# Gate rows of every third quad made one slab earlier, h stores four slabs behind the load, and the input stage's waits and time-step chain moved

## The chip, the cores and the metric

The kernel runs on one core of one Trainium2 chip. The metric is the device time of one execution in microseconds (us). The profile is one execution taken by the hardware profiler. TensorE is called PE, VectorE DVE, ScalarE ACT, GpSimd POOL and SyncE SP; each works through its own list of instructions in order and waits on semaphores.

## The reference, cut to what matters

A block of two layers over 256 tokens of width 2048. Layer 0 mixes with a Mamba-2 (SSD) scan, layer 1 with sliding-window attention; both add attention over a memory of 256 tokens, and both end with a PEER layer that picks 128 of 16384 experts for each token.

```python
for l in range(2):
    if l == 0:
        proj = x @ w_in_a                     # 1536 z | 2560 conv input | 24 time steps | 512 memory queries
        main = mamba2_mixer(...)              # conv, silu; dt = softplus(dt_raw + dt_bias); scan; gate; norm
    else:
        main = sliding_window_attention(...)
    x = layer_norm(ALPHA * x + concat(main, memory_attention(...)) @ w_out[l])
    # PEER
    sc = einsum('bshtd,htkd->bshtk', (x @ peer_wq).reshape(...), subkeys)
    top_s, top_i = top_k(sc, 16)              # twice: for each half, then over the 256 sums
    idx, gate = ...                           # 8 heads x 16 experts for each token
    hid = einsum('td,tkd->tk', x, u[idx])
    act = gelu(hid) * gate
    x = layer_norm(ALPHA * x + einsum('tk,tkd->td', act, v[idx]))
```

## The kernel before, in words

**Slabs and pieces.** All weights come from HBM as slabs of 128 partitions x 2048 f32 (1 MB), each made of two pieces of 1024. Every f32 operand is split into a high and a low part of type fp32r: ACT copies a piece from `raw` into `wh` (`hi`, line 512), DVE subtracts and writes `wl` (`lo`, line 1297), and PE multiplies with both (line 854). `raw` has three slab slots, `wh` and `wl` four piece slots, so `hi(p)` waits until PE has used piece p - 4, `lo(p)` follows `hi(p)`, and PE follows `lo(p)`. SP loads slab n when DVE has split slab n - 3 (line 410). A slab of a "t" stage (`slab_t`) takes 16 pairs of a matmul with `wh` and one with `wl`; in the middle of the next slab PE adds the part that ACT copied into `cross` (`fold`), and only then ACT evacuates the slab from PSUM.

**Stages, in order, with their place in the profile.** Memory keys and values (0 to 105 us, 16 slabs), input projection (117 to 332, 36 slabs), SSD scan and memory attention, output projection, query projection, then the experts of layer 0: 128 U slabs (578 to 1284) and 128 V slabs (1284 to 1868). Layer 1 does the same with its own attention; its U slabs run from 2236 to 2937 and its V slabs to 3523.

**Start of the input stage.** Before it, PE multiplies x with the 24 time-step columns (`dtw_r`) and transposes the memory values (line 1137), ACT copies them out (763, 765), and SP stores them to `kv_scratch` (442, 443), since the output of the input stage (`proj`) takes their place. ACT and DVE wait for that store (`spill_done`) and only then split the first pieces. After 20 of the 36 slabs PE stops to transpose the time steps (line 1144, for which DVE copies PSUM into `dt_c`), and DVE computes the input of softplus (1679 to 1683) and goes on with the convolution (1695, 1698), whose operations alternate with two `lo` each.

**U slabs.** PE computes all 128 hidden values for 192 of the 256 tokens in dense form. The other 64 tokens are done by gathers: POOL gathers rows of u, DVE takes 64 dot products (`dot`, line 1462). The first 64 slabs run beside the top-k search; their outputs (`h_kept`) stay in SBUF. Slabs 64 to 127 form eight trips of eight slabs, the spread stage. Their gelu (line 649) writes `hring`, of which two slots are used here, and SP stores each to `h_scratch` (line 456); gelu of slab k waits for the store of slab k - 2. The dense gates are made there, in 48 quads of four tokens, six quads a trip: DVE builds two one-hot tiles (`hot`, line 1580), ACT multiplies one by the gate (`gate_rows`, four operations, line 663), PE multiplies both (`spread`, when the piece of `Q_PIECE` in the trip has been used), ACT copies the gates out (`gates_out`, line 655), and DVE multiplies the kept hidden values (`gate_kept`, line 1573). `hot` has two slots. In ACT's list for slab s of a trip stand: `cross` of slab s - 1, `hi` of piece 2s + 2, gelu of slab s - 1, `hi` of piece 2s + 3, at most one `gates_out`, at most one `gate_rows`.

```python
Q_PIECE = (2, 4, 7, 10, 12, 15)
GATE_SLAB = tuple((p + 1) // 2 - 1 for p in Q_PIECE)     # 0, 1, 3, 4, 5, 7
STORE_LAG = 5
```

SP issues, for each U slab k, the load of slab k and then the store of slab k - STORE_LAG, which waits for that slab's gelu.

## Time and profile before

| | us |
|---|---|
| device time, median of 3 runs | 3527.97 |
| lowest and highest run | 3519.58, 3531.91 |
| profiled execution, device time | 3539.45 |
| profiled execution, span from first to last instruction | 3537.6 |
| busy in that span: PE, DVE, ACT, POOL | 3378.0, 2786.6, 1914.3, 449.6 |

The mean granted clock of PE in the profiled execution is 0.985 of full speed. The busy time of PE is modelled: its matmuls are pipelined, so the gaps between them are a safer reading than their lengths. In the timeline, a figure in brackets is how long the engine sat idle ahead of a row, and what ended it.

### The profile page before, as it was taken

What the parts mean: (1) busy time and instruction counts of PE and PEld (TensorE: products, weight loads), DVE (VectorE), ACT (ScalarE), POOL (GpSimd) and SP (SyncE); (2) the same over time, 40 slices, a digit from 0 to 9 for tenths busy, and PEclk for the clock granted to TensorE, in tenths of its full rate; (3) what the DMA queues carried; (4) which work ended last, traced back from release to release, by engine and by line L of the source; (5) the groups of instructions that cost most, each with busy time, mean ns of one, the idle gap of its engine ahead of it and who ended that gap; (6) DMA issues with size and microseconds to landing.
All of it is one profiled execution on the core that took longest, in us unless ns stands there. A gap on an engine that the chain in (4) does not pass through costs nothing.

```text
span 3537.6 us, 51772 instructions
## 1 busy us (share of the span) xinstructions
PE 3378.0 (95%) x19476; PEld 3020.1 (85%) x19476; DVE 2786.6 (79%) x3856; ACT 1914.3 (54%) x3350; POOL 449.6 (13%) x264
## 2 busy tenths in 40 slices
PE   9999899999999899999998999999999999999998
PEld 7887678998999888888887777999999998888887
DVE  4455556999898878889886555799988887888997
ACT  4445445554666555555555455555566665555555
POOL 0000000001112112222210000001122121222320
PEclk9999999999999999999999899999999999999999
DMA  6443044678899889999984324568889998999995
GB/s 251 162 169 139 33 169 174 224 275 324 314 348 344 313 299 355 355 361 376 377 333 158 119 81 157 191 220 305 317 327 342 331 337 321 359 351 363 379 382 221
DMA packets 169062, 968.86 MB, mean 274 GB/s; under 512 B 18896, under 2 KB 52688, under 8 KB 55376
## 3 DMA queue, kind: packets, MB, share of 16 engines
q1 hardware_dynamic: 132048, 698.61, 53.2%
q0 software_dynamic: 36864, 268.45, 20.8%
q8 instruction: 70, 1.15, 0.1%
q14 instruction: 80, 0.66, 0.1%
HBM read 951.26 MB, written 15.73 MB: 273 GB/s over the span
## 4 chain that ended last, share of the span: by engine, by line
PE 66%; DVE 20%; DMA 8%; ACT 4%; issue 1%; SPq 0%; DVEq 0%; ACTq 0%
PE ps L854 65%; DVE wl L1297 9%; DMA h_scratch<-hring 7%; DVE arena L1462 3%; ACT wh L512 2%; DMA raw<-in_u 1%; ACT hot L663 0%; DVE arena L1514 0%; DVE arena L1524 0%; DVE arena L1504 0%; DVE arena L1520 0%; DMA arena<-in_v,idx 0%; DVE arena L1499 0%; ACT xx L636 0%; DVE arena L1498 0%
## 5 line engine op out<-in xcount | busy, mean ns | idle before, releaser
L1297 DVE TENSOR_TENSOR wl<-raw,wh 128x1024 fp32r<-128x1024 f32 x1264 | 1525.8, 1220 | 604.4 <-ACT wh L512 601.3
L854 PE MATMUL ps<-xx,wh 128*128 128x384 f32 (+1 forms) x5504 | 1716.6, 373 | 51.8 <-DVE wl L1297 29.2
L512 ACT ACTIVATE wh<-raw 128x1024 fp32r<-128x1024 f32 x1264 | 1333.5, 1057 | 619.8 <-PE ps L854 497.3
L854 PE MATMUL ps<-xx,wl 128*128 128x192 f32 (+1 forms) x5504 | 1424.9, 259 | 0.0
L854 PE MATMUL ps<-wh,act 128*128 128x512 f32 x3584 | 1189.0, 389 | 2.8 <-DVE act L1320 2.8
L854 PEld LDWEIGHTS ps<-xx,wh 128*128 128x128 f32 x5504 | 1038.2, 189 | 122.8 <-DVE wl L1297 36.7
L854 PEld LDWEIGHTS ps<-xx,wl 128*128 128x128 f32 x5504 | 1053.3, 191 | 0.3
L854 PE MATMUL ps<-wl,act 128*128 128x512 f32 x2304 | 897.0, 389 | 0.0
L854 PEld LDWEIGHTS ps<-wh,act 128*128 128x128 f32 x3584 | 673.4, 188 | 143.8 <-DVE wl L1297 3.5
L854 PEld LDWEIGHTS ps<-wl,act 128*128 128x128 f32 x2304 | 432.9, 188 | 89.7
L1268 POOL DMA_INDIRECT arena<-in_v,idx x128 | 262.1, 2047 | 843.9 <-DVE arena L1635 821.5
L1268 POOL DMA_INDIRECT arena<-in_urows,idx x128 | 180.1, 1407 | 1174.0 <-DVE arena L1462 843.1
L1635 DVE SCALAR_TENSOR_TENSOR arena<-arena,hid 128x2048 f32<-128x2048 f32 x128 | 300.1, 2344 | 4.0 <-DMA arena<-in_v,idx 3.9
L1462 DVE SCALAR_TENSOR_TENSOR arena<-arena 128x2048 f32<-128x2048 f32 x128 | 292.3, 2283 | 0.0
L541 ACT ACTIVATE cross<-ps 128x192 fp32r<-128x192 f32 (+1 forms) x344 | 117.4, 341 | 318.9 <-PE ps L854 318.5
L649 ACT ACTIVATE hring<-ps 128x192 f32<-128x192 f32 x128 | 42.3, 331 | 262.5 <-DMA h_scratch<-hring 176.6
L854 PE MATMUL ps<-arena 64*128 64x128 f32 (+8 forms) x664 | 117.0, 343 | 21.7 <-ACT arena L810 5.8
L854 PE MATMUL ps<-hot 128*128 128x128 f32 x768 | 106.7, 282 | 28.6 <-ACT hot L663 28.6
L1276 POOL MEMSET xx<- 128x2048 f32 x2 | 3.6, 1805 | 999.5 <-ACT arena L545 999.5
L649 ACT ACTIVATE arena<-ps 128x192 f32<-128x192 f32 x128 | 42.3, 330 | 153.0 <-PE ps L854 149.6
L854 PEld LDWEIGHTS ps<-hot 128*128 128x128 f32 x768 | 94.0, 193 | 35.6 <-ACT hot L663 35.6
L854 PEld LDWEIGHTS ps<-arena 64*128 64x128 f32 (+4 forms) x664 | 78.5, 181 | 51.5 <-issue 20.3
(210 smaller groups left out, 1790.7 us busy)
## 6 DMA issues: line engine op xcount, KB each, us to landing
raw<-in_u SPq DMA_DIRECT2D x256, 1024.0 KB
raw<-in_v SPq DMA_DIRECT2D x256, 1024.0 KB
raw<-in_w SPq DMA_DIRECT2D x119, 1024.0 KB
h_scratch<-hring SPq DMA_DIRECT2D x128, 96.0 KB
hring<-h_scratch SPq DMA_DIRECT2D x128, 96.0 KB
arena<-in_memT SPq DMA_DIRECT2D x4, 512.0 KB, 6.4
arena<-in_xT SPq DMA_DIRECT2D x4, 512.0 KB, 7.8
arena<-in_urows,idx POOLq DMA_INDIRECT x128
```

The lines of the kernel that those rows point to most:

```text
L512: nc.scalar.activation(wh[:, j, :], raw_piece(p), ACT.Copy).then_inc(hi_ready, 1)
L541: nc.scalar.activation(cross[:, 0:n], ps[:, bank, n:2 * n], ACT.Copy).then_inc(cross_out, 1)
L649: nc.scalar.activation(h_kept[:, k, :] if kept else hring[:, j, :], ps[:, j, 0:ND], ACT.Gelu).then_inc(evac_done, 1)
L854: return nc.tensor.matmul(out, lhs, rhs, start=start, stop=stop, **kw)
L1268: pool.indirect_dma_start(out=gbuf[n % SLOTS], out_offset=None, in_=rows_of, in_offset=bass.IndirectOffsetOnAxis(ap=idx[:, j:j + 1], axis=0))\
L1276: nc.gpsimd.memset(xx[:, :, :, 0:NS].bitcast(F32), 0.0).then_inc(xz_ready, 1)
L1297: v.tensor_tensor(wl[:, j, :], raw_piece(p), wh[:, j, :].bitcast(F32), ALU.subtract).then_inc(lo_ready, 1)
L1462: v.scalar_tensor_tensor(out=rows_u, in0=rows_u, scalar=1.0, in1=xrep, op0=ALU.mult, op1=ALU.mult, accum_out=hid[:, j:j + 1]).then_inc(slo ...
L1635: v.scalar_tensor_tensor(out=vacc, in0=rows_v, scalar=hid[:, j:j + 1], in1=vacc, op0=ALU.mult, op1=ALU.add).then_inc(slot_free, 1)
```

## The change

Three edits, independent of one another.

1. `GATE_SLAB` becomes 0, 1, 2, 4, 5, 6: of the six quads in a trip, the third and the last have their gate rows made one slab earlier. Nothing is added.
2. `STORE_LAG` goes from 5 to 4: SP issues the store of slab k - 4, not k - 5, after the load of slab k, and waits for that slab's gelu there.
3. In the input stage ACT and DVE split the first four pieces ahead of the wait for the spill, DVE copies `dt_c` there too, and the two calls of PE's stage (20 and 16 slabs) become one; the transposes of the time steps stand at the end of its second slab, and DVE's time-step operations after its eighth piece. The 36 pieces that follow come as one row, so each convolution group of DVE has four more pieces ahead of it.

```diff
-GATE_SLAB = tuple((p + 1) // 2 - 1 for p in Q_PIECE)
+GATE_SLAB = tuple(p // 2 - 1 for p in Q_PIECE)
-STORE_LAG = 5
+STORE_LAG = 4
@@ ACT, after the memory stage @@
+        for j in range(RING):
+            hi(P_INA + j, j)
         for n in range(4):
             act.wait_ge(vtr_ready, n + 1)
...
-        t_stage(P_INA, T_INA, S_INA, copy_out(lambda k: proj[:, k, LPAD:LPAD + TOK]))
+        t_stage(P_INA, T_INA, S_INA, copy_out(lambda k: proj[:, k, LPAD:LPAD + TOK]), done=RING)
@@ PE, t_stage @@
-                       lone=s == 0)
+                       lone=s == 0, then=second if s else None)
@@ PE, input stage @@
-        t_stage(P_INA, T_INA, XBC_C, 2)
-
-        pe.wait_ge(dtc_evac, 1)
-        for t in range(NT):
-            last = nc.tensor.transpose(ps[:, 7, t * P:(t + 1) * P], dt_c[:, t * P:(t + 1) * P], ident)
-        last.then_inc(dt_ready, 1)
-        t_stage(P_INA + 2 * XBC_C, T_INA + XBC_C, S_INA - XBC_C, 2)
+        def turn_dt(e):
+            if e == 1:
+                pe.wait_ge(dtc_evac, 1)
+                for t in range(NT):
+                    last = nc.tensor.transpose(ps[:, 7, t * P:(t + 1) * P], dt_c[:, t * P:(t + 1) * P], ident)
+                last.then_inc(dt_ready, 1)
+
+        t_stage(P_INA, T_INA, S_INA, 2, second=turn_dt)
@@ DVE, input stage @@
+        for j in range(RING):
+            lo(P_INA + j, j)
+        dve.wait_ge(dtc_ready, 1)
+        v.tensor_copy(dt_c, ps[:, 6, 0:TOK]).then_inc(dtc_evac, 1)
         dve.wait_ge(spill_done, 32)
...
-        split_t(P_INA, XBC_C)
-
-        dve.wait_ge(dtc_ready, 1)
-        v.tensor_copy(dt_c, ps[:, 6, 0:TOK]).then_inc(dtc_evac, 1)
+        split_t(P_INA, RING, done=RING)
         dve.wait_ge(dt_ready, 1)
...
+        split_t(P_INA + 2 * RING, XBC_C - RING + BODY // 2)
...
-                for j in (2 * k, 2 * k + 1):
-                    lo(i * (2 * BODY) + (P_INA + 2 * XBC_C + j), j % RING)
+                for j in (i * 2 * BODY + RING + 2 * k, i * 2 * BODY + RING + 2 * k + 1):
+                    if j < 2 * (S_INA - XBC_C):
+                        lo(P_INA + 2 * XBC_C + j, j % RING)
```

ACT in the first trip of the spread stage, from its list for slab 2 of the trip: `wh` is `hi`, `hring<-ps` gelu, `arena<-ps` `gates_out`, `hot` `gate_rows`. Before:

```order
586 L512 ACTIVATE wh<-raw 128x1024
587 L649 ACTIVATE hring<-ps 128x192
588 L512 ACTIVATE wh<-raw 128x1024
589 L655 ACTIVATE arena<-ps 128x64x4
590 L541 ACTIVATE cross<-ps 128x192
591 L512 ACTIVATE wh<-raw 128x1024
592 L649 ACTIVATE hring<-ps 128x192
593 L512 ACTIVATE wh<-raw 128x1024
594 L655 ACTIVATE arena<-ps 128x64x4
595 L663 ACTIVATE hot<-hot,par 128x128 x4
596 L541 ACTIVATE cross<-ps 128x192
```

And now:

```order
586 L512 ACTIVATE wh<-raw 128x1024
587 L649 ACTIVATE hring<-ps 128x192
588 L512 ACTIVATE wh<-raw 128x1024
589 L655 ACTIVATE arena<-ps 128x64x4
590 L663 ACTIVATE hot<-hot,par 128x128 x4
591 L541 ACTIVATE cross<-ps 128x192
592 L512 ACTIVATE wh<-raw 128x1024
593 L649 ACTIVATE hring<-ps 128x192
594 L512 ACTIVATE wh<-raw 128x1024
595 L655 ACTIVATE arena<-ps 128x64x4
596 L541 ACTIVATE cross<-ps 128x192
```

The four operations of the third quad moved ahead of the `cross` copy, two splits and a gelu.

DVE from the end of x's low part to the start of the convolution. Before:

```order
12 L1659 MEMSET arena 128x128
13 L1662 MEMSET arena 128x20x3
14 L1665 CAST arena<-ident_r 128x128
15 L1667 TENSOR_SCALAR par<-par 128x12
16 L1668 TENSOR_SCALAR arena<-arena 128x128
17 L1669 CAST tri_r<-arena 128x128
18 L1670 CAST tri_r<-arena 128x128
19 L1297 TENSOR_TENSOR wl<-raw,wh 128x1024 x40
20 L1674 COPY arena<-ps 128x256
21 L1679 TENSOR_TENSOR arena<-ps,par 128x48
```

And now (the lines are three to five further down in the changed file):

```order
12 L1662 MEMSET arena 128x128
13 L1300 TENSOR_TENSOR wl<-raw,wh 128x1024 x4
14 L1666 COPY arena<-ps 128x256
15 L1669 MEMSET arena 128x20x3
16 L1672 CAST arena<-ident_r 128x128
17 L1674 TENSOR_SCALAR par<-par 128x12
18 L1675 TENSOR_SCALAR arena<-arena 128x128
19 L1676 CAST tri_r<-arena 128x128
20 L1677 CAST tri_r<-arena 128x128
21 L1300 TENSOR_TENSOR wl<-raw,wh 128x1024 x4
22 L1683 TENSOR_TENSOR arena<-ps,par 128x48
```

Four splits and the copy of `dt_c` moved ahead of the wait for the spill (which stands before the memset of 128x20x3), and the time-step operations from behind 40 splits to behind eight.

SP at the passage from the U slabs to the V slabs of layer 0. Before:

```order
142 L410 DMA raw<-in_v 128x2048
143 L456 DMA h_scratch<-hring 128x192
144 L410 DMA raw<-in_v 128x2048
145 L456 DMA h_scratch<-hring 128x192 x3
146 L410 DMA raw<-in_v 128x2048
```

And now:

```order
144 L410 DMA raw<-in_v 128x2048
145 L456 DMA h_scratch<-hring 128x192
146 L410 DMA raw<-in_v 128x2048
147 L456 DMA h_scratch<-hring 128x192 x2
148 L410 DMA raw<-in_v 128x2048
```

Each store stands one load further forward; two stores, not three, follow the third V slab.

## Rows read from the trace of the kernel before

**Rows 1.** Windows: length, busy PE, PEld, DVE, ACT, POOL, clock, DMA share, GB/s

```profile
914.00:1284.60 370.60, 350.93 (x2494) 345.67 (x2493) 317.80 (x318) 223.14 (x487) 73.94 (x48) 0.99 0.91 330
1284.00:1868.00 584.00, 582.10 (x2561) 481.50 (x2560) 502.53 (x520) 326.71 (x515) 125.59 (x62) 1.00 0.93 353
1199.00:1210.00 11.00, 6.77 (x30) 6.54 (x30) 6.35 (x8) 4.08 (x10) 1.89 (x2) 0.69 0.69 249
1278.00:1290.00 12.00, 9.41 (x40) 8.06 (x40) 5.77 (x8) 6.51 (x12) 0.00 (x0) 0.72 0.43 154
```

**Rows 2.** PE's waits, spread stage of layer 0 (us in total, times, longest)

```profile
PE ps L854 <- ACT hot L663: 14.1, 15, 4.2
PE ps L854 <- ACT hring L649: 2.8, 3, 2.1
PE ps L854 <- DVE arena L1573: 2.0, 1, 2.0
```

**Rows 3.** The same for the spread stage of layer 1

```profile
PE ps L854 <- ACT hot L663: 14.5, 15, 3.0
PE ps L854 <- ACT hring L649: 2.6, 3, 1.2
PE ps L854 <- DVE act L1320: 1.4, 1, 1.4
```

**Rows 4.** Timeline, start of the input stage (start, length, instruction, idle ahead)

```profile
105.03 0.37 ACT L545 ACTIVATE arena<-ps 128x256 f32<-128x256 f32 x1
...
107.69 1.91 PE L1137 MATMUL ps<-ident_r,arena 128*128 128x128 f32 x16
...
114.37 3.90 ACT L512 ACTIVATE wh<-raw 128x1024 fp32r<-128x1024 f32 x4 [3.04 <-DMA kv_scratch<-arena]
...
116.78 0.76 PE L854 MATMUL ps<-xx,wh 128*128 128x512 f32 x1 [7.19 <-issue]
...
120.65 0.40 PE L854 MATMUL ps<-xx,wh 128*128 128x512 f32 x1
...
121.00 0.39 PE L854 MATMUL ps<-xx,wh 128*128 128x512 f32 x1
```

**Rows 5.** Timeline, input stage after 20 of its 36 slabs

```profile
233.43 0.21 DVE L1679 TENSOR_TENSOR arena<-ps,par 128x48 f32<-128x48 f32 x1 [6.62 <-PE ps L1144]
...
237.49 0.77 PE L854 MATMUL ps<-xx,wh 128*128 128x512 f32 x1 [4.09 <-issue]
...
243.38 0.40 PE L854 MATMUL ps<-xx,wh 128*128 128x512 f32 x1
```

**Rows 6.** Timelines of PE, ACT and DVE around two third quads, layer 0

```profile
1060.35 1.27 ACT L663 ACTIVATE hot<-hot,par 128x128 f32<-128x128 f32 x4
...
1061.67 1.16 PE L854 MATMUL ps<-hot 128*128 128x128 f32 x8 [0.52 <-ACT hot L663]
...
1097.96 1.22 DVE L1580 TENSOR_TENSOR hot<-iota,sel_t 128x1024 f32<-128x1024 f32 x1
...
1099.03 0.38 ACT L655 ACTIVATE arena<-ps 128x256 f32<-128x256 f32 x1
```

**Rows 7.** Timelines of ACT, SP and PE around one late h store, layer 0

```profile
1186.20 0.33 ACT L649 ACTIVATE hring<-ps 128x192 f32<-128x192 f32 x1
...
1188.77 0.33 SPq L410 DMA_DIRECT2D raw<-in_u  x1
1189.14 0.43 SPq L456 DMA_DIRECT2D h_scratch<-hring  x1
...
1200.72 0.33 ACT L649 ACTIVATE hring<-ps 128x192 f32<-128x192 f32 x1 [4.87 <-DMA h_scratch<-hring]
...
1203.47 2.08 PE L854 MATMUL ps<-hot 128*128 128x128 f32 x8 [4.23 <-ACT hot L663]
```

**Rows 8.** DMA issues of the whole program (count, KB each, median us to landing)

```profile
kv_scratch<-arena SPq DMA_DIRECT2D x2, 512.0 KB, 3.1
```

**Rows 9.** Timeline, end of the U slabs of layer 0

```profile
1279.50 0.33 ACT L649 ACTIVATE hring<-ps 128x192 f32<-128x192 f32 x1 [6.76 <-DMA h_scratch<-hring]
```

More of the change, by code:

```diff
@@ L885, in slab_t, with t_stage @@
                     then(e)
-        def t_stage(p0, t0, n, x_count, closed=True):
+        def t_stage(p0, t0, n, x_count, closed=True, second=None):
             lead = t0 == 0
```

## The prediction

> **What bounds the kernel now.** I read first how each stage's span divides, then what PE waited for in it, then the timeline at the two places of the input stage where the diff works. In the spread stage of layer 0 PE is busy 350.9 of 370.6 us, DVE 317.8, ACT 223.1, and the DMA engines 0.91 of the time at 330 GB/s [rows 1]. So PE sets the pace there too, and only what it idles can be gained: the V slabs, where it is busy 582.1 of 584 us [rows 1], have nothing to give. What it waits for is small in number. Fifteen times in each layer it waits for `hot`, the gate rows of ACT, 14.1 and 14.5 us in all; three times in each for gelu's output in `hring`, 2.8 and 2.6; and at the passage to the V slabs 2.0 and 1.4 [rows 2, 3]. The `hot` waits come some 22 us apart, every four slabs, which is at the third and the last quad of each trip and at no other: exactly the two that edit 1 moves.
>
> Why those two: ACT can't do gelu of slab s - 1 before PE's fold in the middle of slab s, and behind gelu stand a split, a `gates_out` and the rows. The rows of a third quad end at 1060.35 + 1.27 = 1061.62, and PE starts on them at 1061.67 after 0.52 us of idling [rows 6]. This is the usual case. The costly ones have a second cause: gelu waits for the store of two slabs before. Gelu of 1186.20 is stored by a DMA that SP issues only at 1189.14, since the load of the next slab goes first and that waits for DVE; the gelu that needs the slot runs at 1200.72 after 4.87 us of waiting, its gate rows follow, and PE stands 4.23 us [rows 7].
>
> In the input stage PE idles twice. At its start it ends the transposes at 109.60 and begins at 116.78, since ACT splits only when the spill has landed, at 114.37 [rows 4]. After slab 20 it idles 4.09 us: DVE waits 6.62 us for the time-step transposes, then does the time steps and a group of the convolution, and only then the split that PE needs [rows 5]. Both times PE comes back at the lower of its two clocks, 1.2 instead of 2.4 GHz: one pair of matmuls in the normal state takes 0.35 us (120.65 to 121.00), while the six before 120.65 took 3.87 us and the nine after 237.49 took 5.89 us [rows 4, 5].
>
> **The change part by part.** The sum is made against the profiled execution (3537.6 us of span, 3539.45 of device time); the median of the runs is 11.5 us below that, and I take the same saving off it.
>
> *Input stage, start.* The three loads for these pieces are issued while the memory stage runs. ACT is free at 105.03 + 0.37 = 105.40, so its four splits (3.90 us) end at 109.3 [rows 4], DVE's about a us behind. PE needs only the first piece at 109.60, and has two slabs of 16 x 0.35 = 5.6 us, till 120.8, before it needs anything that waits for the spill. The price: ACT copies the memory values out behind its splits, so the spill starts later by at most 109.3 - 107.7 = 1.6 us and ends at 116.0. A `cross` copy and the fifth piece's two halves of the split (about 2.6 us together) follow, at 118.6. The cover is 2.2 us, so this costs nothing; without it PE would lose one for one what is missing. Gain: 7.2 us of idling and 3.87 - 6 x 0.35 = 1.8 us of low clock, 9.0 together.
>
> *Input stage, slab 20.* Nothing stops PE there any more. The transposes are in slab 1, for which `dt_c` was copied long before; DVE waits there for PE, with four pieces ahead of it done, and its five small operations take about 1 us beside 5.8 us a slab. The convolution groups (about 2.1 us) with two splits (2.3 us) fit into a slab as before, and the last two groups end behind the last split but ahead of PE's end. Gain: 4.1 us of idling and 5.89 - 9 x 0.35 = 2.7 us of low clock, 6.8 together. Input stage in all: 15.8 us.
>
> *Gate rows.* The four operations are the same, 1.27 us, one slab earlier. Can ACT start them there? They need the one-hot of DVE, which for the third quad ends at 1097.96 + 1.22 = 1099.18, while the `gates_out` ahead of them in the new order ends at 1099.41 [rows 6]: just in time. Queued behind them are the `cross` copy and the splits of the next slab; these start up to 1 us later, but the split is for a piece that PE needs two slabs on. What goes: 14.1 + 14.5 = 28.6 us.
>
> *Stores.* With four slabs behind, SP issues the store as soon as gelu is done, ahead of the next load. In [rows 7] that is at about 1186.6, not 1189.14, and without the 1 MB of the load of 1188.77 in front. Does SP's new wait hold back that load? No: it needs the split of a piece that ACT makes only after the same gelu. The load has 96 KB more ahead of it, 0.3 us at 330 GB/s. How early the store lands no row shows; the bounds are the 2.5 us of earlier issue alone, and, if the load is what it waits for, 2.5 us and the load's own 3.2 us (1 MB at 330 GB/s), 5.7 in all. A 512 KB store in quiet landed 3.1 us after its issue [rows 8], against 11.5 us here, so queueing is most of it and I take the upper end. By that 4.87 is gone, and of the 6.76 us at the end of the U slabs [rows 9] one is left. What goes: the `hring` waits, 5.4 us; at the passages 2.0 and 1.4 [rows 2, 3]; and the low clock that follows a long stall, which is 0.31 and 0.28 of two windows of 11 and 12 us [rows 1], 3.4 us each, of which I count 3 and 3, since a part lies in the idling itself. Together 14.8 us.
>
> The Trainium skill, page "DMA: Bandwidth & Descriptors", section "Queues, rings and completion order", says that each DMA engine takes the descriptors of one ring in order; that is the queueing that the edit shortens, and [rows 7, 8] agree. The same page's section "Anatomy of one DMA — SWDGE (gpsimd) path" speaks against it: about 2 us of each DMA are a fixed cost, most of it the receipt of the write, which no place in the queue shortens; by that, an estimate, the 11.5 us would hold 9.5 that can shrink, which is still more than 5.7, and the sum would be the same.
>
> Sum of what PE loses in the spread stages: 28.6 + 14.8 = 43.4 us. I don't expect all of it. With the long waits gone DVE is next: its 318 us of work have to fit into some 350, and it runs in bursts (a dot product, a one-hot and two splits in one slab), so now and then a row or a split will be late by some tenths; and the DMA engines go from 0.91 towards 0.96. I take off an eighth, which is 0.17 us for each of the 32 moved quads, and get 38. With the input stage: 15.8 + 38 = **54 us**. From 3539.45 that is 3485; from the median 3528 it is **3474**.
>
> **The rivals.**
> *Half of the gate waits stay.* If DVE's one-hot comes late in its new place, ACT waits there, in order, and hands the delay on to splits and gelu; PE then waits again, in another place. For it: in [rows 6] the margin is 0.2 us, and DVE has 0.86 load. Against it: the margin is that small only because ACT starts on time; where ACT itself comes late, the one-hot is there. Half of 43.4 is 22, and the time 3528 - 16 - 22 = 3490.
> *The DMA engines become the bound.* The stage moves 330 GB/s at 0.91; the V slabs, with more of the same, reach 353 at 0.93 [rows 1]. If 0.93 is all there is, a stage of 370.6 us can shrink only by the factor 0.91/0.93, 8 us a layer; 16 and 16 give 3496. Against it: 353 GB/s is 7% above 330, and I ask for 6%.
> *Slower than before.* DVE falls behind for good: for each moved quad ACT stands still with the splits behind it, longer than the half us that PE idles today. The input stage gives 16 us, so this decides from 0.5 us (today's wait) + 16/32 = 1.0 us for each quad; at 1.5 us it would give 3528 - 16 + 32 = 3544. It needs a DVE without reserve, and its idle share of 0.14 speaks against.
> *The change doesn't do what it says.* If PE's start in the input stage hung on something other than the split (the trace names no releaser there, only "issue"), 9 us would stay: 3483. It lies within the range.
>
> **How the numbers follow.** The forecast, 3474 with its own range of 3460 to 3488, has 0.68, of which the case of the held input start is a part with 0.05. The DMA bound and half the gate waits have 0.08 and 0.15, both faster by more than 0.3%. Slower has 0.03. The rest, 0.06, is a wash by several small causes, with the input stage alone at 3512 on its faster side. A measurement of this kernel tells no less than about 0.3%, 10.6 us. So faster 0.94, same 0.03, slower 0.03. The range goes down to 3460, where all 59 us come and the runs scatter as today's (3520 to 3532), and up to 3497, which takes in both rivals.
>
> **What the next profile would show.** Right: PE's first matmul of the input stage within 1 us of the last transpose, no idling after slab 20, PE's wait for `hot` under 5 us in all instead of 28.6, gelu's wait for `h_scratch` a fourth or less of what it was, the stage at about 350 us, and clock windows like those two gone. Wrong: ACT waiting for `hot` of DVE (the one-hot too late); PE waiting for `wl` (DVE the bound); gelu still waiting for stores at a DMA share above 0.95; or `raw` late for ACT in the U slabs.

## The result and the profile after

| | us |
|---|---|
| changed kernel, median of 4 runs | 3472.47 (3470.97 to 3474.34) |
| kernel before beside it, median of 4 runs | 3527.61 (3519.58 to 3531.91) |
| ratio, 95% interval | 0.9847, 0.9828 to 0.9865 |
| profiled execution of the changed kernel, device time and span | 3473.37, 3471.6 |

The change saves 55.1 us. Forecast were 54 and a time of 3474. The profiled executions lie 66 us apart, since the one of before was 11.5 us over its median and the one of after is 0.9 over its own.

The lines of the code are two or three further down than in the profile before (gelu is still L649, but PE's matmul is L856, DVE's split L1300, its dot product L1465, the one-hot L1583). First the windows of the changed kernel: from the first matmul on `hot` to the first matmul on `act`, of layer 0 and of layer 1, and the V slabs of layer 0 behind it. The columns are those of [rows 1]: length, busy time of PE, PEld, DVE, ACT and POOL, granted clock, DMA share, GB/s.

```profile
894.50:1239.40 344.90, 344.20 (x2513) 344.06 (x2512) 318.90 (x320) 230.23 (x492) 77.67 (x48) 1.00 0.94 357
2526.10:2871.00 344.90, 344.19 (x2513) 344.05 (x2512) 319.00 (x320) 230.23 (x492) 77.98 (x48) 1.00 0.94 357
1239.40:1824.50 585.10, 581.15 (x2560) 480.19 (x2560) 502.54 (x518) 326.68 (x515) 138.04 (x62) 1.00 0.93 353
```

Against [rows 1]: PE idles 0.7 us in the whole spread stage instead of some 20, at full clock, and the two layers now take the same time to 0.1 us. The transfers reach 357 GB/s at a share of 0.94. The V slabs are what they were (585.1 and 584.0 us).

The waits in the spread stage of layer 0 (us in total, times, longest), to be read against [rows 2]:

```profile
ACT hring L649 <- PE ps L856: 84.4, 64, 3.4
ACT hot L663 <- DVE hot L1583: 2.1, 8, 0.4
```

PE no longer appears there with a wait for `hot` or `hring`. Gelu waits 64 times, once a slab, and each time for PE, never for a store. ACT does wait for DVE's one-hot in its new place, but eight times and 0.4 us at the most.

The start of the input stage, the timeline of all engines in the columns of [rows 4]:

```profile
107.92 1.91 PE L1139 MATMUL ps<-ident_r,arena 128*128 128x128 f32 x16
...
109.59 0.48 PE L856 MATMUL ps<-xx,wh 128*128 128x512 f32 x1
...
111.77 0.43 SPq L443 DMA_DIRECT2D kv_scratch<-arena  x1
...
117.93 0.38 ACT L541 ACTIVATE cross<-ps 128x256 fp32r<-128x256 f32 x1 [5.61 <-DMA kv_scratch<-arena]
...
118.37 0.39 PE L856 MATMUL ps<-cross,ident_r 128*128 128x256 f32 x1 [0.21 <-ACT cross L541]
```

PE starts at 109.59, right behind its transposes, 7.2 us sooner than in [rows 4]. But the second spill, behind which SP issues loads of w from 112.25 on, takes 6.1 us to land, and PE's fold in the middle of its second slab stands 0.21 us for the `cross` copy behind it: the cover was used up to the last. The 4.09 us after slab 20 [rows 5] are gone.

### The profile page after: what moved, and what is told of

It reads as the page before. It is cut to its first block, busy times and chain, and to the rows that moved or that the text cites. A ratio compares the mean times of both kernels' runs of the same rounds, so it can differ in the third digit from the quotient of the medians.

```text
span 3471.6 us, 51777 instructions
## 1 busy us (share of the span) xinstructions
PE 3359.3 (97%) x19476; PEld 3012.7 (87%) x19476; DVE 2785.4 (80%) x3856; ACT 1924.4 (55%) x3350; POOL 476.5 (14%) x264
## 4 chain that ended last, share of the span: by engine, by line
PE 78%; DVE 17%; DMA 2%; ACT 2%; issue 1%; DVEq 0%; SPq 0%; ACTq 0%
PE ps L856 77%; DVE wl L1300 7%; DVE arena L1465 2%; DMA arena<-in_v,idx 1%; ACT wh L512 1%; DMA raw<-in_v 1%; DVE arena L1517 0%; DVE arena L1527 0%; DVE arena L1507 0%; DVE arena L1523 0%; DVE arena L1502 0%; DVE arena L1501 0%; ACT xx L636 0%; DVE arena L1638 0%; DVE arena L1485 0%
## 5 line engine op out<-in xcount | busy, mean ns | idle before, releaser
L1300 DVE TENSOR_TENSOR wl<-raw,wh 128x1024 fp32r<-128x1024 f32 x1264 | 1528.0, 1222 | 550.8 <-ACT wh L512 549.7
L856 PE MATMUL ps<-xx,wh 128*128 128x384 f32 (+1 forms) x5504 | 1709.6, 372 | 35.1 <-DVE wl L1300 29.6
L856 PE MATMUL ps<-xx,wl 128*128 128x192 f32 (+1 forms) x5504 | 1422.6, 258 | 0.0
L856 PE MATMUL ps<-wh,act 128*128 128x512 f32 x3584 | 1188.5, 389 | 4.1 <-DVE act L1323 4.1
L856 PEld LDWEIGHTS ps<-xx,wh 128*128 128x128 f32 x5504 | 1034.8, 188 | 102.3 <-DVE wl L1300 36.8
L856 PEld LDWEIGHTS ps<-xx,wl 128*128 128x128 f32 x5504 | 1050.2, 191 | 0.3
L856 PE MATMUL ps<-wl,act 128*128 128x512 f32 x2304 | 896.4, 389 | 0.0
L856 PEld LDWEIGHTS ps<-wh,act 128*128 128x128 f32 x3584 | 672.7, 188 | 145.8 <-DVE wl L1300 5.6
L856 PEld LDWEIGHTS ps<-wl,act 128*128 128x128 f32 x2304 | 432.5, 188 | 89.5
L1271 POOL DMA_INDIRECT arena<-in_v,idx x128 | 279.7, 2185 | 822.4 <-DVE arena L1638 802.0
L1271 POOL DMA_INDIRECT arena<-in_urows,idx x128 | 189.4, 1480 | 1118.1 <-DVE arena L1465 787.2
L1465 DVE SCALAR_TENSOR_TENSOR arena<-arena 128x2048 f32<-128x2048 f32 x128 | 292.8, 2288 | 0.7 <-DMA arena<-in_urows,idx 0.7
L856 PE MATMUL ps<-arena 64*128 64x128 f32 (+8 forms) x664 | 117.0, 343 | 21.2 <-ACT arena L812 5.8
L649 ACT ACTIVATE hring<-ps 128x192 f32<-128x192 f32 x128 | 42.3, 330 | 168.8 <-PE ps L856 166.6
L649 ACT ACTIVATE arena<-ps 128x192 f32<-128x192 f32 x128 | 42.3, 330 | 153.3 <-PE ps L856 150.0
L663 ACT ACTIVATE hot<-hot,par 128x128 f32<-128x128 f32 x384 | 122.4, 393 | 4.2 <-DVE hot L1583 4.2
L856 PEld LDWEIGHTS ps<-arena 64*128 64x128 f32 (+4 forms) x664 | 78.6, 181 | 50.9 <-issue 20.3
L1583 DVE TENSOR_TENSOR hot<-iota,sel_t 128x1024 f32<-128x1024 f32 x96 | 117.2, 1221 | 1.2 <-ACT sel_t L704 1.2
```

Of the source, the lines that this page charges most:

```text
L649: nc.scalar.activation(h_kept[:, k, :] if kept else hring[:, j, :], ps[:, j, 0:ND], ACT.Gelu).then_inc(evac_done, 1)
L663: nc.scalar.activation(row1, row1, ACT.Copy, scale=gate_t[:, 4 * q + t:4 * q + t + 1])\
L856: return nc.tensor.matmul(out, lhs, rhs, start=start, stop=stop, **kw)
L1271: pool.indirect_dma_start(out=gbuf[n % SLOTS], out_offset=None, in_=rows_of, in_offset=bass.IndirectOffsetOnAxis(ap=idx[:, j:j + 1], axis=0))\
L1300: v.tensor_tensor(wl[:, j, :], raw_piece(p), wh[:, j, :].bitcast(F32), ALU.subtract).then_inc(lo_ready, 1)
L1465: v.scalar_tensor_tensor(out=rows_u, in0=rows_u, scalar=1.0, in1=xrep, op0=ALU.mult, op1=ALU.mult, accum_out=hid[:, j:j + 1]).then_inc(slo ...
```

## The experiments

Each stretch below is read in the same way from a profiled execution: the **spread stretch** from the first matmul on `hot` to the first on `act`, in layer 0 and layer 1; the **head** is when it starts in layer 0, so that it holds the input stage and all that stands between. The medians come from timed runs, beside runs of the kernel before on the same chip; where two kernels in one text stand beside other runs of before, the ratio is the surer number.

| kernel | median us (range, runs) | ratio to before [95%] | spread stretches | head |
|---|---|---|---|---|
| before | 3527.61 (3519.6 to 3531.9, 4) | | 373.0 / 367.7 | 911.6 |
| changed | 3472.47 (3471.0 to 3474.3, 4) | 0.9847 [0.9828, 0.9865] | 344.9 / 344.9 | 894.5 |
| gate rows alone | 3528.29 (3518.2 to 3538.8, 12) | 1.0001 [0.9987, 1.0015] | 367.3 / 366.2 | 911.7 |
| stores alone | 3507.27 (3502.9 to 3511.3, 6) | 0.9944 [0.9929, 0.996] | 355.9 / 356.0 | 912.6 |
| input stage alone | 3515.67 (3501.5 to 3527.2, 12) | 0.9965 [0.995, 0.9981] | 375.8 / 364.1 | 898.1 |
| gate rows and stores | 3483.04 (3481.9 to 3486.5, 4) | 0.9877 [0.9857, 0.9896] | 344.9 / 344.9 | 911.2 |
| input start alone | 3527.35 (3510.3 to 3538.7, 12) | 0.9976 [0.9957, 0.9995] | 372.0 / 368.9 | 902.2 |
| half the gate rows, stores | 3496.17 (3493.7 to 3499.5, 4) | 0.9901 [0.9875, 0.9926] | 350.1 / 350.3 | 911.4 |

The windows of before over the same stretches, in the columns of [rows 1]:

```profile
911.60:1284.60 373.00, 353.33 (x2513) 348.07 (x2511) 320.09 (x320) 225.36 (x492) 73.94 (x48) 0.99 0.91 330
2569.70:2937.40 367.70, 349.04 (x2514) 343.93 (x2512) 320.54 (x320) 225.37 (x492) 72.59 (x48) 1.00 0.91 335
```

### Gate rows alone (g_only)

The kernel before, with one edit:

```diff
-GATE_SLAB = tuple((p + 1) // 2 - 1 for p in Q_PIECE)
+GATE_SLAB = tuple(p // 2 - 1 for p in Q_PIECE)
```

> The kernel before with the gate-row edit alone (slabs 0, 1, 2, 4, 5, 6). Theory A (two causes on PE's wait for hot: the rows' place, about 0.5 us for each of 30 quads, and late gelus from late h stores on top; moving the rows cuts both, since a late gelu now has a whole slab to spare, but leaves PE's waits for hring, the passages to the V slabs and part of the low clock): 3527.6 - 27 = 3501, PE's wait for hot under 3 us, gelu's wait for h stores still over 100 us. Rival B (the h stores are the whole cause, the rows only hand their delay on): under 8 us gained, 3520 or more, the hot waits turned into waits elsewhere. Rival C (the rows' place is the whole cause): the full 40 us of the two edits, 3488.

Measured: nothing, 1.0001 with a half width of 0.0014. That is Rival B of the expectation: under 8 us, and the waits turned into waits elsewhere. Yet the edit does exactly what it says; PE's waits for `hot`, 28.6 us in 30 times in the whole of before, are no longer there. The waits of the whole program in this kernel:

```profile
ACT hring L649 <- DMA h_scratch<-hring: 239.4, 88, 5.0
PE ps L854 <- ACT hring L649: 17.4, 26, 2.7
```

The same view of before:

```profile
ACT hring L649 <- DMA h_scratch<-hring: 176.6, 72, 6.8
...
PE ps L854 <- ACT hot L663: 28.6, 30, 4.2
```

Gelu's wait for its store has grown by 62.8 us, and PE waits for gelu's output instead of for the gate rows. So the largest term of my sum, 28.6 us, was time that PE had to lose anyway: something slower than PE went round beside it. The chain of waits of before shows what, over two slabs of layer 0 (start, length, what):

```profile
1017.00 9.50 DMA h_scratch<-hring
...
1026.58 0.04 ACT hring L649
...
1026.80 1.06 ACT wh L512
...
1027.89 1.24 DVE wl L1297
...
1029.14 0.33 SPq L410
...
1029.82 6.76 DMA h_scratch<-hring
...
1036.66 0.04 ACT hring L649
```

It is a closed loop, and in these rows PE isn't in it. A store lands; the gelu that waited for its slot runs; behind it ACT makes a split, DVE the other half; SP, which has the load for that buffer ahead of the store, issues the load, and only then gelu's store, here 3.3 us after the slot came free (1026.5 to 1029.8). With two slots one turn of the loop serves two slabs. PE's pace of 344.9/64 = 5.39 us a slab allows a turn of 10.8 us, and so a landing of 7.5 if the rest takes 3.3. These rows show landings of 9.50 and 6.76. An estimate for the whole stage, as if every turn were like this one: 367.7/64 x 2 = 11.5 us a turn, which leaves 8.2 for the landing. The chain itself holds 26 landings in the two stretches of before, of 6.76 to 16.52 us and 9.3 on average; only stores that decide the time stand there.

Not every turn is like this one. DVE's list is part of the loop: where DVE is behind, the load and the store after it wait through its dot products and one-hots too. The rows of the same chain just ahead of the store of 1017.00:

```profile
1013.24 2.21 DVE arena L1462 x2
...
1015.46 1.15 DVE wl L1297
...
1016.62 0.33 SPq L410
```

In the chain over the spread stretch of layer 0, with the gate rows moved, 37.7% of the time are landings of h stores, 44.4% DVE's work and 5.0% PE. In before the shares are 28.9, 15.7 and 42.9%: there PE, gelu and the late gate rows take the lead for some 20 us at a time, and the store's loop in between. So two rounds stood one beside the other. Moving the rows took one of them away, and the other alone is no faster: 367.3 and 366.2 us, against 373.0 and 367.7 in a profiled execution of before that was itself 11.5 us over the median. A third slot in the kernel before, which would loosen the loop and leave the order of SP's list alone, was not run.

### Stores alone (s_only)

The kernel before, with `STORE_LAG = 4` for 5.

> The kernel before with the store lag of 4 alone. Theory A: PE's waits for hot fall to 0.5 us each, 30 x 0.5 = 15 us in all, those for hring and the stall at the passage go, gelu's wait for h stores falls from 177 us to under 20: 3527.6 - 23 = 3505. Rival B: 3488, all of it. Rival C: no change, 3524 to 3528. If the lag gains only by its 2.5 us of earlier issue, gelu's wait keeps a third of its 177 us, some 60.

Measured: 20.5 us off the median, 3507 where Theory A had 3505, and stretches of 355.9 and 356.0. The waits of the whole program:

```profile
ACT hring L649 <- PE ps L854: 181.5, 128, 3.4
...
PE ps L854 <- ACT hot L663: 15.2, 30, 0.5
```

All 128 gelus wait for PE now and none for its store, and the wait for `hot` comes down from 28.6 us to 15.2 without the gate rows being touched, its longest from 4.2 to 0.5. SP's own waits show what was cut: in the stretch of layer 0 it waited 296.5 us for DVE's splits and 10.9 for gelu before, and now 139.2 and 175.8. The store no longer stands behind DVE's list. Two things follow. Half of what I had put down to the gate rows was the store's doing, since a late gelu makes the rows late. And with the loop gone the gate rows do set the pace: 355.9 - 344.9 = 11.0 us of a stretch fall on 16 quads, 0.69 us each, of which the waits show 0.5 as idle. The window of this stretch, in the columns of [rows 1], has the rest:

```profile
912.60:1268.50 355.90, 347.59 (x2513) 343.97 (x2511) 320.28 (x320) 226.95 (x492) 72.37 (x48) 1.00 0.93 346
```

The same number of matmuls is busy 347.6 us here and 344.2 in the changed kernel, and PE is idle 8.3 us for 0.7. So of the 11.0 us the profile lists 7.6 as idle and 3.4 as longer matmuls.

### Both, without the input stage (gs)

> The kernel before with both spread-stage edits and the old input stage. Theory A: they overlap by about 14 us of hot waits that either removes, so 27 + 23 - 12 = 38 to 40: 3488. Rival B or C: equal to the better of the two alone within 3 us. If the input stage's edit is independent of the two, gs and i_only together give the 55 us of the whole change within 3 us.

Measured: 3483.04, 44.7 us off, where Theory A had 38 to 40, and against 20.5 + 0 for the two alone. The edits are independent in the code and not in what they bring. PE's list is now the only bound, 344.9 us in both layers. So the gate rows are worth nothing by themselves and 24 us once the stores are out of the way; the stores are worth 20.5 by themselves. These two numbers depend on the order in which the edits are made; only the 44.7 doesn't.

### Half of the gate rows (g3_s)

With `STORE_LAG = 4` and only one of the two late quads in each trip moved:

```diff
-GATE_SLAB = tuple((p + 1) // 2 - 1 for p in Q_PIECE)
+GATE_SLAB = (0, 1, 2, 4, 5, 7)
```

> The kernel before with store lag 4 and only the third quad of each trip moved (slabs 0, 1, 2, 4, 5, 7). With lag 4 the stretch from the first to the V slabs' start takes 355.9 us with no quad moved and 344.9 with both. Theory (with the stores out of the way PE's own list is the bound, and each unmoved quad costs it the same 0.69 us): 350.4 us in both layers, 3495. Rival (one late quad is enough to hold the stage, since slabs follow each other in one loop): 355 or more. Second rival (the last quad, with its gates copied out in the next trip, is the dear one): not in the middle.

Measured: stretches of 350.1 and 350.3, in the middle of 344.9 and 356 as eight quads of 0.69 us make it (350.4), and a median of 3496.17, between 3483.0 and 3507.3. Once PE is the bound its small waits add up one by one.

### Input stage alone, and its start alone (i_only, start_only)

Input stage alone is the changed kernel with `GATE_SLAB` and `STORE_LAG` as before. The start alone is the kernel before, with the first four splits ahead of the wait for the spill, and PE's two calls and the time steps left where they were:

```diff
@@ ACT @@
+        for j in range(RING):
+            hi(P_INA + j, j)
...
@@ DVE @@
+        for j in range(RING):
+            lo(P_INA + j, j)
...
-        split_t(P_INA, XBC_C)
+        split_t(P_INA, XBC_C, done=RING)
```

> The changed kernel with the gate rows and the store lag as before, so the input stage's edit alone. Theory A: 3527.6 - 16 = 3512, PE's first matmul of the input stage at about 109.6, no stall after slab 20, the rest of the trace as before (its spread stages also give a second look at those of the kernel before: some 365 to 370 us for the stretch that took 370.6). Rival: the earlier start is given back before the experts (the SSD stage waits for the convolution or for the time steps): under 8 us, 3520.

> The kernel before with the first half of the input stage's edit alone: ACT and DVE split the first four pieces ahead of the wait for the spill; the time-step chain stays behind slab 20. Theory (the two gaps are independent): PE starts at 109.6 instead of 116.8, about 9 us of span up to slab 20, and the stall after slab 20 stays at 4.1 us with its low clock: 3527.8 - 9 = 3519. Rival (the spill or the copy of the memory values comes so much later that PE stands at its first fold): under 4 us, 3524.

The sharpest measure is where PE ends the stage, at its last fold. In before and in the changed kernel:

```profile
331.74 0.38 PE L854 MATMUL ps<-cross,ident_r 128*128 128x256 f32 x1 [0.47 <-ACT cross L541]
```

```profile
315.76 0.38 PE L856 MATMUL ps<-cross,ident_r 128*128 128x256 f32 x1 [0.47 <-ACT cross L541]
```

The five profiles with the old input stage have this row at 331.07 to 332.37, the eight with the new one at 315.51 to 315.80: 16.0 us on average, for 15.8 forecast. The start alone has it at 323.08, so it is worth 8.5 for 9.0 forecast, and the time-step chain the other 7.4 for 6.8. The start alone keeps the stop after slab 20, whose row in its timeline of PE is that of [rows 5] again:

```profile
229.07 0.76 PE L856 MATMUL ps<-xx,wh 128*128 128x512 f32 x1 [4.09 <-issue]
```

Most of it is still there at the head: 911.2 to 912.6 with the old input stage, 894.5, 895.5, 895.6, 897.6 and 898.1 with the new one and the old search stage, so 13.5 to 17.1 us, and 902.2 with the start alone. By the trace Theory A holds for both kernels.

The medians are less clear. The ratio of the whole edit makes 12.3 us (6.7 to 17.6), that of the start alone 8.5, with anything from 1.8 to 15.2, and the bare medians of the start and of before lie only 2.6 apart. The table shows why: the kernels whose spread stage waits for the store's loop scatter over 12 to 28 us, those bound by PE over 3 to 9 (in fewer runs, 4 to 6 and not up to 23). A gain of 9 us drowns in the one. Between two kernels bound by PE, gate rows and stores (3483.0) and the changed kernel (3472.5, and 3468.6 in the second group of runs, below), the input stage is worth 10.6 and 14.4 us by the medians, and 10.6 and 18.3 by the ratios to before.

### One slot for gelu's output (one_slot)

How early does the store land in its new place? In the changed kernel nobody waits for it. With one slot in place of two, every gelu waits for the store ahead of it, and its landing is laid bare. The changed kernel, with:

```diff
-HOUT = 2
+HOUT = 1
@@ ACT, gelu @@
-                        act.wait_ge(h_stored[j], 16 * stores)
-                nc.scalar.activation(h_kept[:, k, :] if kept else hring[:, j, :], ps[:, j, 0:ND],
+                        act.wait_ge(h_stored[0], 16 * stores)
+                nc.scalar.activation(h_kept[:, k, :] if kept else hring[:, 0, :], ps[:, j, 0:ND],
```

> The changed kernel with one slot of hring instead of two, so that gelu of slab k waits for the store of slab k - 1, issued right after its gelu: the time from a store's issue to its landing in its new place ahead of the load shows as gelu's wait. Theory (queueing behind the load of the slab was most of the 8 to 11 us that a store took): 4 to 7 us from issue to gelu's release, stretch 64 x (that + 0.5): 290 to 480, so the PE bound of 345 or somewhat more. Rival (a store to HBM takes 8 us or more wherever it stands, and the gain came from the 2.5 us of earlier issue alone): 64 x 8.5 = 545 us for the stretch, 3870 in all.

One execution took 3550.38 us, with stretches of 384.9 and 382.0. Its chain of waits in layer 0 (start, length, what):

```profile
1009.49 6.91 DMA h_scratch<-hring
...
1016.48 0.34 ACT hring L649
...
1016.84 5.92 DMA h_scratch<-hring
...
1022.85 0.34 ACT hring L649
...
1023.20 8.20 DMA h_scratch<-hring
```

The store is issued 0.4 us behind its gelu, not 3.3. The chain holds 78 landings in the two stretches, of 2.88 to 8.48 us and 6.2 on average, against the 9.3 of before. An estimate over the whole stage gives a little less: a turn takes 384.9/64 = 6.0 us, which leaves 5.6 for the landing where the same estimate for before left 8.2 (48 of the 64 gelus of layer 0 waited for their store, ten for PE). The second profile of the changed kernel, which lists a time for these stores (number, KB each, median us from issue to landing), agrees:

```profile
h_scratch<-hring SPq DMA_DIRECT2D x128, 96.0 KB, 5.6
```

From a gelu to its slot's coming free the estimates make 3.3 + 8.2 = 11.5 us before and 6.0 now, so 5.5 us less: near the upper of my two bounds, 5.7. Worked out from that, with two slots each loop has 10.8 us of PE's time for its 6.0, a reserve of 4.8 us where in before 0.7 were lacking. The rival, that a store in this place lands hardly sooner, would have made the stretch much longer still. What shortens the landing is not shown as well as that it is shorter. The loads of before are issued 0.4 to 0.7 us ahead of the store. The three stores above were issued 0.9, 2.3 and 4.2 us behind a load, and took 6.91, 5.92 and 8.20 us, so the distance to the load isn't all.

### A store still one load earlier (lag3)

The changed kernel with `STORE_LAG = 3`.

> The changed kernel with a store lag of 3: SP waits for gelu of slab k - 3 ahead of the load of slab k + 1, a slab later than that load could go. Theory: the loads go out up to 3 us later but `raw` has more to spare than that, so PE's list remains the bound: stretch of 344.9 to 347 us in both layers, 3472 to 3477. Rival (the wait ahead of the load is what costs): ACT waits for `raw` in the U slabs, stretch over 352, 3487 or more.

Measured: 3475.47 (3475.14 to 3482.23), ratio 0.9846 [0.982, 0.9872], stretches 346.9 and 348.6. It is the changed kernel with 2.0 and 3.7 us lost in the stretches. The waits of ACT in the whole program, where the changed kernel has 0.4 us for `raw<-in_u` (2.5 in its second profile):

```profile
ACT wh L512 <- DMA raw<-in_u: 54.7, 48, 3.1
```

SP's own waits in the spread stretch of layer 0 show why (each store waits for its gelu, and the loads behind it have little left to wait for):

```profile
SPq L456 <- ACT hring L649: 290.3, 64, 7.8
SPq L410 <- DVE wl L1300: 10.9, 13, 4.0
```

And its timeline, a store and the load that it had held:

```profile
1003.62 0.33 SPq L456 DMA_DIRECT2D h_scratch<-hring  x1
1003.99 1.23 SPq L410 DMA_DIRECT2D raw<-in_u  x1
```

SP waits for the gelu of slab k - 3, and the load of the next slab stands behind it. The time is the theory's (3472 to 3477), the wait for `raw` is the rival's sign, at a small price. So four slabs is a place between two costs: at five the store waits for the load, at three the load waits for the store.

### More of DVE's work in the spread stage (seven_dots, seven_even, four_moved)

PE is at its floor in the spread stage, so the next gain would be to move dot products from the search stage ahead of it, where they cost PE time, into the spread stage. That also asks whether DVE, busy 319 of 345 us, has a reserve. Three forms, each the changed kernel with another table; `UNIT_DOTS`, the dot products of the search stage, shrinks from 16 to 8, 8 and 12.

```diff
-DOT_PIECE = (2, 5, 8, 10, 13, 15)
+DOT_PIECE = (0, 2, 5, 7, 10, 12, 15)                                # seven_dots
+DOT_PIECE = (0, 2, 5, 7, 10, 12, 14)                                # seven_even
+DOT_PIECE = ((2, 5, 8, 10, 12, 14), (0, 2, 5, 7, 10, 12, 14))       # four_moved
```

> The changed kernel with seven dot products in each trip of the spread stage instead of six (pieces 0, 2, 5, 7, 10, 12, 15), and eight instead of sixteen beside the top-k search: 17.7 us of DVE's work moved from the search, where DVE is the bound and PE idles some 10 us a layer, into the spread stage, where DVE has 318 us of work in 342. Theory (a mean of 336 in 342 is too full for work that comes in bursts): the search gains 8 to 10 us a layer, the spread stage loses 5 to 15; 3463 to 3482. Rival (only the sum counts): 18 us faster, 3455. Rival (DVE has no reserve in the spread stage, as the slower case of the prediction has it): spread stage over 365 us, 3490 or more.

> As seven_dots, with the seven dot products of a trip spread evenly (pieces 0, 2, 5, 7, 10, 12, 14), since there DVE waited 14 and 18 us a layer for gathered rows, 15 or 16 times, mostly after dots one piece apart. Theory (those waits, and not DVE's full list, took the spread stage from 345 to 358): 348 to 352, 3465. Rival (DVE's list of 336 us in 345 is the limit): 355 to 360 again, 3476.

> The changed kernel with four dot products moved instead of eight: six (pieces 2, 5, 8, 10, 12, 14) and seven (0, 2, 5, 7, 10, 12, 14) in turn, twelve beside the search. Theory (DVE has a reserve of some 25 us in the spread stage, of which bursts take part): the search gains 5 us a layer and the spread stage stays within 3 us of 344.9: 3466. Rival (any more work for DVE there costs as much as it saves): 3472.

| kernel | median us (range, runs) | ratio to before [95%] | spread stretches | head |
|---|---|---|---|---|
| eight moved | 3477.18 (3472.8 to 3494.6, 4) | 0.9862 [0.983, 0.9893] | 355.9 / 361.0 | 884.7 |
| eight moved, evenly | 3490.85 (3482.8 to 3494.7, 4) | 0.9886 [0.9852, 0.9921] | 362.8 / 365.3 | 885.5 |
| four moved | 3479.80 (3469.1 to 3489.8, 6) | 0.9856 [0.9828, 0.9885] | 351.9 / 356.4 | 892.4 |
| changed, second group of runs | 3468.62 (3466.5 to 3473.0, 6) | 0.9825 [0.9801, 0.985] | 344.9 / 344.9 | 897.6 |

The search stage gains what was asked of it: the head is 10 to 13 us earlier for eight dot products. The spread stage gives back more. Its waits in layer 0, with eight moved:

```profile
ACT hot L663 <- DVE hot L1583: 18.2, 20, 2.1
...
DVE arena L1465 <- DMA arena<-in_urows,idx: 13.8, 15, 3.2
...
PE ps L856 <- DVE wl L1300: 6.3, 13, 1.7
```

The same stretch with the eight spaced evenly:

```profile
DVE arena L1465 <- DMA arena<-in_urows,idx: 19.6, 22, 1.8
...
PE ps L856 <- DVE wl L1300: 11.1, 18, 1.6
```

DVE waits for the gathered rows of a dot product, ACT for DVE's one-hot, and PE for DVE's half of the split. I had thought that the uneven spacing of the first form was the cause; the even one is worse, 362.8 for 355.9, so that fell. Only the first form lies where its Theory had it (3463 to 3482). With four moved, Theory (within 3 us of 344.9) fell as well: 351.9 and 356.4.

The chain over the stretch of layer 0 says what took its place. Evenly spaced, 39.9% of it are landings of gathered rows, 52.5% DVE's work and 5.0% PE; unevenly 27.1, 52.0 and 18.7%. It is the same kind of loop as the store's: POOL gathers into two slots and starts the next gather when a dot product has freed one, DVE waits for the landing, and its list passes the delay on. Two rows of the even form's chain:

```profile
1008.17 10.60 DMA arena<-in_urows,idx
...
1018.80 2.30 DVE arena L1465 x2
```

Such a landing and its dot product make 13 us a turn for two dot products, where PE's pace leaves 2 x 344.9/56 = 12.3 with seven in a trip, and 14.4 with six. That is an estimate from the long landings of the chain; the median of all is 9.3, which would fit. The work of DVE in the stretch had grown from 318.9 us to 334.0 with eight moved, in 355.9. Which of the two weighs more, the landing or DVE's load, these runs don't settle; a third slot was not tried. The changed kernel was timed once more, beside the same runs of before as the even form, the four moved and the one slot; it stands in the table's last line:

> The changed kernel once more, on the same chip as the three beside it: 3472 within 4 us, stretches of 344.9 us in both layers again.

It gave 3468.62 beside 3529.33, 60.7 us, and the same stretches to the tenth: no version here beats the change for certain, and the three medians are 9 to 22 us above it. The two groups put the gain between 55 and 61 us.

## Why the prediction was right, and where it was not

**The time and its sum.** 3474 forecast, 3472.5 measured; 54 us of gain, 55.1 measured. The parts of the sum hold less well than the sum, and that it came within 1.1 us is in part luck: the spread stages were forecast at 38 us and gave 44.7, the input stage at 15.8 and gave 16.0 at its end, which makes 60.7 together. The second group of runs gives just that, the first 55.1, and between the two lies the scatter of before.

**What bounds the kernel now.** "PE sets the pace there too, and only what it idles can be gained" was wrong in its first half, and it is the step that failed. Two rounds stood above PE's list: the store's loop with DVE's list in it, 367.3 and 366.2 us a stretch when it is alone, and PE with the late gate rows, 355.9 and 356.0 when that is alone. PE's list, 344.9, was the floor underneath. That is why the sum came near: the edits together took away everything that stood above the floor, and PE's distance to the floor is what I had summed up. Had the change held only edit 1, the same working would have given 28.6 us (or seven eighths of it), and the chip gives 0 +- 5.

**Gate rows, 28.6 us.** Mis-sized: 0 alone, 24 us behind the stores (44.7 - 20.5). The long ones among the waits, those up to 4.2, belonged to late stores, which I had seen and said of [rows 7], but put into the sum under the gate rows all the same. Without them 15.2 us remain as idle, and 22 (32 x 0.69) as time.

**Stores, 14.8 us.** Mis-sized in the other direction: 20.5 alone. The bounds of the landing held, and the upper end that I took, 5.7 us, is what one slot lays bare, 5.5. SP's wait doesn't hold the next load at four slabs, as I had worked out from the split behind gelu; at three it does. The wait of 6.76 us at the end of the U slabs [rows 9], of which I let one stand, went altogether, and so did the stretches at low clock: the clock is 1.00 in both layers.

**The eighth taken off.** Not needed. ACT waits 2.1 us for DVE's one-hot, PE 0.7 us for anything. That 44.7 came where I had 38, and even above my ceiling of 43.4, has one more cause beside the scatter of before: a stall of PE costs more than the idle time that the profile shows for it, 0.69 for 0.5, or 0.19 x 32 = 6 us over both layers. In before PE is busy 353.3 and 349.0 us in the two stretches with the work that takes 344.2 now, 14 us in all, of which I had counted 6 as low clock.

**Input stage, 15.8 us.** Size and mechanism hold: 16.0 us at the end of the stage, 8.5 for 9.0 at its start and 7.4 for 6.8 at slab 20; the medians can't tell it as closely. The step on the cover doesn't hold: I had the spill ending at 116.0, the work behind it at 118.6, and PE's need at 120.8, the third slab. The first need is the fold in the middle of the second slab, 118.16, and the second spill, issued at 111.77 and now sharing the DMA engines with the loads of w, took 6.1 us and ended at 117.9. PE stood for 0.21 us there. I had taken the cover for 2.2 us where nothing was left.

**The rivals.** *Half of the gate waits stay*: refuted, 0.4 us is the longest wait for the one-hot (0.7 in the second profile). *The DMA engines become the bound* at 0.93: refuted by 0.94 and 357 GB/s at PE's floor, and 367 at 0.95 with eight dot products moved. *Slower*, with DVE without reserve: it didn't come, but it stood nearer than its 0.03 says: eight more dot products a layer (15 us of DVE's time) bring its sign, ACT waiting 18.2 us for the one-hot, and cost the stretches 11 to 20 us, though the landing of the gathered rows has its part in that. *The change doesn't do what it says*: refuted by the first matmul at 109.59.

**The Trainium skill.** The page "DMA: Bandwidth & Descriptors", section "Queues, rings and completion order", has the descriptors of one ring taken in order, and says in the same place that a later one may finish its write before an earlier one. The runs agree with both. A store that isn't issued right behind the load lands sooner, after about 5.6 us and not 8.2 by the estimates above. But being first in the queue doesn't keep a store free of what follows: between 111.77 and 117.90 the changed kernel moved 317 GB/s, 1.9 MB, of which the two spills are at most 1.05, so some 0.9 MB of the loads issued behind them went beside them. The section "Anatomy of one DMA — SWDGE (gpsimd) path" is on DMAs that GpSimd issues, and these stores are issued by SP; that its fixed cost of about 2 us holds for them, as the prediction had it, no run here shows. The shortest landing seen is 2.88 us.

## What to carry to other kernels

Before the idle time of the busiest engine is shared out among the waits that end it, look in the chain of waits for a closed loop that goes round without that engine: through a buffer's slot, a store and a queue in order. If its turn is longer than the engine's pace, the engine's other waits are slack against it: mending them alone brings little or nothing (here 0 +- 5 us for 28.6), and the gain of mending all is the distance to the engine's own list. And where two edits meet at one floor, time them alone and together: a null result for one alone says nothing of its worth behind the other.

## What the runs showed of the hardware that I had not expected

- **A small store behind a large load.** The 96 KB stores that decide the time land after 6.8 to 16.5 us (9.3 on average) when issued some 0.4 us behind a 1 MB load of the same queue, and after 2.9 to 8.5 (6.2 on average) when issued ahead of the slab's load, at 320 to 335 GB/s in both. The place isn't all: with the same order, the medians of all such stores are 5.6 us in the changed kernel, and 7.3 and 7.6 with four and with eight evenly spaced dot products moved.
- **Loads behind a store slow it too.** The two 512 KB spills took 3.1 us (median) in quiet [rows 8], and 4.4 in the changed kernel, where 1 MB loads are issued half a us behind the second, which took 6.1.
- **PE's short stalls cost more than they show.** Waits of 0.5 us at 16 quads lengthened a stretch by 11.0 us, 0.69 each, and at eight by 5.3. Of the 11.0 us, 7.6 are listed as idle and 3.4 as longer matmuls.
- **The scatter went with the bound.** Kernels that wait for a DMA round a loop, the store's or the gathers', scatter over 12 to 28 us between executions (0.3 to 0.8%, 4 to 23 runs), those bound by PE's list over 3 to 9 (4 to 6 runs), with stretches that repeat to 0.2 us between the layers.
